# A two-layer hybrid decoder step on one core: token groups of 512, 512 and 64 in both MLPs instead of 384, 384 and 320

## What is computed

```python
x = x + m                                  # m: the token mixer's output
h = rmsnorm(x, norm_mlp[layer])
x = x + jnp.square(jax.nn.relu(h @ w_up[layer])) @ w_down[layer]
```

## Time and profile before

| | before |
|---|---|
| median of 3 runs | 2856.1 us |
| span of the profiled execution | 2853.2 us |
| TensorE matmul busy | 2650.3 us, 93% |
| TensorE weight load busy | 2527.7 us, 89% |
| VectorE busy | 1397.6 us, 49% |
| GpSimd busy | 852.2 us, 30% |
| ScalarE busy | 629.0 us, 22% |
| mean granted TensorE clock | 0.951 of full |

### The profile page before, as it was taken

The page is one execution under the profiler, slowest core; times in us unless marked ns, Lnnn a source line. Parts: engine busy times, 40 slices in busy tenths (PEclk is TensorE's granted clock), DMA queues, the critical chain, the costliest instruction groups (busy, mean ns, idle before and its releaser), DMA issues.

```text
span 2853.2 us, 38633 instructions
## 1 busy us (share of the span) xinstructions
PE 2650.3 (93%) x15232; PEld 2527.7 (89%) x15232; DVE 1397.6 (49%) x2168; ACT 629.0 (22%) x1086; POOL 852.2 (30%) x383
## 2 busy tenths in 40 slices
PE   5988987999999999998989999897999999999996
PEld 5978756999999999998978888787999999999996
DVE  3656444643443344346566767653643443344344
ACT  3050124130110011003232525342220110011002
POOL 2332101433333333333211111112433333333331
PEclk9999978999999999999979999887999999999998
DMA  3111002111111111112101111102111111111111
GB/s 119 40 31 53 23 24 100 45 38 45 45 45 45 45 45 45 45 45 77 60 24 45 40 37 40 39 30 100 45 38 45 45 45 45 45 45 45 45 45 70
DMA packets 36849, 137.63 MB, mean 48 GB/s; under 512 B 5697, under 2 KB 6337, under 8 KB 35409
## 3 DMA queue, kind: packets, MB, share of 16 engines
q1 hardware_dynamic: 28368, 103.56, 10.9%
q10 hardware_dynamic: 8320, 31.70, 2.9%
HBM read 120.36 MB, written 14.88 MB: 47 GB/s over the span
## 4 chain that ended last, share of the span: by engine, by line
issue 55%; PE 29%; POOL 14%; DVE 1%; POOLq 1%; DMA 0%; ACT 0%; DVEq 0%; ACTq 0%; SPq 0%
PE PS L457 29%; POOL WH L437 8%; POOL WL L440 6%; DVE X L1533 0%; DMA WR<-ws 0%; DVE RA L1119 0%; POOLq L436 0%; POOLq L448 0%; DVE X L1129 0%; POOLq L439 0%; ACT RS L784 0%; DVE RS L1082 0%; ACT L787 0%; ACT L784 0%; PE PS L507 0%
## 5 line engine op out<-in xcount | busy, mean ns | idle before, releaser
L457 PE MATMUL PS<-RA,WH 128*128 128x384 f32 (+1 forms) x4800 | 1182.5, 330 | 71.4 <-DVE RA L1073 23.9
L457 PE MATMUL PS<-RB,WH 128*128 128x384 f32 (+1 forms) x4272 | 1063.4, 332 | 12.4 <-DVE TR L1115 8.6
L437 POOL TENSOR_TENSOR WH<-WR,ZERO 128x1024 fp32r<-128x1024 f32 x189 | 362.3, 1917 | 1941.6 <-PE PS L457 1938.1
L457 PEld LDWEIGHTS PS<-RA,WH 128*128 128x128 f32 x4800 | 853.1, 189 | 84.1 <-issue 69.2
L457 PEld LDWEIGHTS PS<-RB,WH 128*128 128x128 f32 x4272 | 765.8, 191 | 27.7 <-issue 21.0
L457 PE MATMUL PS<-RA,WL 128*128 128x384 f32 (+1 forms) x2400 | 787.4, 328 | 0.0
L457 PE MATMUL PS<-RB,WL 128*128 128x384 f32 (+1 forms) x2136 | 704.1, 330 | 0.0
L440 POOL TENSOR_TENSOR WL<-WR,WH 128x1024 fp32r<-128x1024 f32 x189 | 489.6, 2591 | 14.8
L457 PEld LDWEIGHTS PS<-RA,WL 128*128 128x128 f32 x2400 | 454.0, 189 | 0.0
L1129 DVE TENSOR_TENSOR X<-PS,X 128x384 f32<-128x384 f32 (+1 forms) x384 | 202.4, 534 | 468.0 <-PE PS L457 468.0
L457 PEld LDWEIGHTS PS<-RB,WL 128*128 128x128 f32 x2136 | 407.0, 191 | 0.0
(11 more groups left out here) (178 smaller groups left out, 1621.2 us busy)
## 6 DMA issues: line engine op xcount, KB each, us to landing
WR<-ws SPq DMA_DIRECT2D x189, 512.0 KB, 3.3
X<-xT ACTq DMA_DIRECT2D x8, 544.0 KB, 8.8
EB<-xT ACTq DMA_DIRECT2D x8, 544.0 KB, 7.9
x_spill<-X ACTq DMA_DIRECT2D x1, 4352.0 KB, 13.1
EB<-x_spill ACTq DMA_DIRECT2D x8, 544.0 KB, 7.1
yT<-X SPq DMA_DIRECT2D x8, 544.0 KB, 2.7
GA<-st_gla ACTq DMA_DIRECT2D x4, 1024.0 KB, 5.6
glas_o<-GA ACTq DMA_DIRECT2D x4, 1024.0 KB, 3.9
```

The lines of the kernel that those rows point to most:

```text
L437: nc.gpsimd.tensor_tensor(WH[:, slot, :], WR[:, slot, :], ZERO[:, 0:1].to_broadcast([P, 1024]), ALU.add).then_inc(w_high, 1)
L457: return nc.tensor.matmul(out, lhsT, rhs, start=start, stop=stop, skip_group_check=True)
```

## The change

A second table is added and used in the MLPs alone: by TensorE in up and down steps (a new parameter `cut` of `group`, `step` and `first_step`), by ScalarE in its square and its copy, and by VectorE in `up` and `down`. The mixers, the 1/rms factor and the final norm stay with `GROUPS`. Three groups, three banks and all semaphore counts stay. In the first up step of an MLP VectorE waits for all three parts of 1/rms before its first group, since the first 512 columns span two parts.

```diff
 GROUPS = [(0, 384), (384, 384), (768, T - 768)]
+MLP_GROUPS = [(0, 512), (512, 512), (1024, T - 1024)]
...
-            def group(n, slot, g, src, tiles, w0, o=0, two=False, after_two=False, signal=2):
+            def group(n, slot, g, src, tiles, w0, o=0, two=False, after_two=False, signal=2, cut=GROUPS):
...
-                s, size = GROUPS[g]
+                s, size = cut[g]
...
-                            first_step(n, RB, parts_of, norm)
+                            first_step(n, RB, parts_of, norm, cut=MLP_GROUPS)
                         else:
-                            step(n, slot, RB, after_two=after_two)
+                            step(n, slot, RB, after_two=after_two, cut=MLP_GROUPS)
...
-                                  o=o, two=True, after_two=after_two or j > 0, signal=1)
+                                  o=o, two=True, after_two=after_two or j > 0, signal=1, cut=MLP_GROUPS)
...
-                        A(TR[:, grp(g)], TR[:, grp(g)], ACT.Square).then_inc(sq_done, 1)
+                        A(TR[:, s:s + size], TR[:, s:s + size], ACT.Square).then_inc(sq_done, 1)
...
-                    for g, (s, size) in enumerate(GROUPS):
+                    for g, (s, size) in enumerate(MLP_GROUPS):
                         if first:
-                            dve.wait_ge(rs_ready, 3 * (norm - 1) + g + 1)
+                            dve.wait_ge(rs_ready, 3 * norm)
...
-                        for g, (s, size) in enumerate(GROUPS):
+                        for g, (s, size) in enumerate(MLP_GROUPS):
                             dve.wait_ge(gemm_done, 6 * n + 3 * o + g + 1)
```

More of the change, by code:

```diff
@@ L474, in group, with step, first_step @@
                 last.then_inc(gemm_done, signal)
-            def step(n, slot, src, after_two=False):
+            def step(n, slot, src, after_two=False, cut=GROUPS):
                 for g in range(3):
-                    group(n, slot, g, src, range(KT), 0, after_two=after_two)
-            def first_step(n, src, f, norm=None, after_two=False, order=range(KT)):
+                    group(n, slot, g, src, range(KT), 0, after_two=after_two, cut=cut)
+            def first_step(n, src, f, norm=None, after_two=False, order=range(KT), cut=GROUPS):
                 slot = n % 2
@@ L486, in first_step @@
                     pe.wait_ge(h_low, 8 * f + at + 1)
-                    for g, (s, size) in enumerate(GROUPS):
+                    for g, (s, size) in enumerate(cut):
                         if at == 0 and n:
@@ L798, in one @@
                 def one(n, v, tile):
-                    for g, (s, size) in enumerate(GROUPS):
+                    for g, (s, size) in enumerate(MLP_GROUPS):
                         act.wait_ge(psum_free, 6 * n + 2 * (g + 1))
-                        A(TR[:, grp(g)], TR[:, grp(g)], ACT.Square).then_inc(sq_done, 1)
+                        A(TR[:, s:s + size], TR[:, s:s + size], ACT.Square).then_inc(sq_done, 1)
                         act.wait_ge(sq_done, v + (g + 1))
-                        A(RA1[:, 0, tile, s:s + size], TR[:, grp(g)], ACT.Copy).then_inc(a_high, 1)
+                        A(RA1[:, 0, tile, s:s + size], TR[:, s:s + size], ACT.Copy).then_inc(a_high, 1)
                 v0 = 96 * layer
@@ L1114, in up @@
                             dve.wait_ge(a_low, v - 2 + g)
-                        V.scalar_tensor_tensor(TR[:, grp(g)], PS[:, g, 0:size], 0.0, RS[:, s:s + size],
+                        V.scalar_tensor_tensor(TR[:, s:s + size], PS[:, g, 0:size], 0.0, RS[:, s:s + size],
                                                ALU.max, ALU.mult).then_inc(psum_free, 2)
-                    for g, (s, size) in enumerate(GROUPS):
+                    for g, (s, size) in enumerate(MLP_GROUPS):
                         dve.wait_ge(a_high, v + g + 1)
-                        V.tensor_tensor(RA1[:, 1, tile, s:s + size], TR[:, grp(g)],
+                        V.tensor_tensor(RA1[:, 1, tile, s:s + size], TR[:, s:s + size],
                                         RA1[:, 0, tile, s:s + size].bitcast(F32), ALU.subtract).then_inc(a_low, 1)
```

## The result

| | before | after |
|---|---|---|
| median | 2856.4 us (4 runs, 2855.9 to 2857.5) | 3074.4 us (4 runs, 3073.8 to 3075.7) |
| ratio, 95% interval | | 1.0765 [1.075, 1.0779] |
| span of the profiled execution | 2853.2 us | 3072.0 us |
| granted TensorE clock, mean | 0.951 | 0.954 |

The change makes the kernel 218 us slower. The forecast was 3076.0 us, 1.6 us above the median.

The account below looks back on a forecast made before the run. TensorE was taken to bound the MLPs, 1514 of 2853 us. Span 2853.2 + 221.2 (short matmuls) + 1.8 (wait) - 2.6 (tail) - 0.5 (last evictions) = 3073.1 us; median 2.9 above, 3076.0; range 3050 to 3125.

Parts of the forecast that it names:

- Columns plus 13.3 ns: TensorE in the MLPs: a matmul costs its columns at 2.4 GHz plus 13.3 ns, unless something slower stands behind it.
- The short matmul: 64-column group in the MLPs: an exposed weight load makes each matmul 112 ns, not 40; 3072 of them, +221.2 us.
- The wait: First up step of each MLP: group 0's eviction waits for all three Exp, TensorE resumes 0.9 us later; +1.8 us.
- The tail's waits: First MLP's tail: two TensorE waits of 1.13 us on VectorE would be gone, up to 1.3 us each, -2.6 us.
- that margin: Down steps: TensorE needs bank 0 again after 6.78 us, 5.94 before; margin grows by 0.8 us, counted as no gain.
- The clock: Rival, short groups of up steps: the clock falls to half, 206 ns per matmul, +144 us more, 3220 us; 6%.
- Loads hidden or cheaper in float32r: Rival, 64-column group: 40 ns per short matmul, 2855 us, 4%; half way, some 67 ns, 2938 us, another 4%.
- faster long matmuls: Rival, 512-column matmuls: the 13.3 ns vanish or shrink; 2773 us with loads hidden, 2994 us with them exposed; 2%.
- the upper bound of 120 ns: 64-column matmul in the MLPs: at most the load and then 13.3 ns on top, +246.7 us.
- Float32r in four passes: Rival, short matmuls: done as float32 with two loads, 224 ns, 3419 us; without a second load 120 ns; 4%.

Follow-up runs that it names:

- the half-load run: The changed kernel, but matmuls of the 64-column group use 64 of their 128 weight columns, except in `first_step`: 2930.2 us, 1.0259 of before.
- the low parts' run: The kernel before, with each low part of an up step written behind the next group's eviction, the last at the end: 2850.8 us, 0.9984 of before.
- the 128- and 192-column cuts: The changed kernel with groups of 512, 448 and 128 columns: 2998.3 us, 1.0499 of before; with 448, 448 and 192: 2924.0 us, 1.0242.

## Why the prediction was right

*The bound and the formula.* TensorE's spacing set the time before and after. Columns plus 13.3 ns held from 256 to 512 columns (120, 147, 173, 187 and 227 ns at 256, 320, 384, 416 and 512), but for the 203 ns at 448.

*The short matmul.* The one term that carried the sum was the 112 ns of a load, taken from float32 loads behind 64 and 8 columns and one pair of float32r loads behind an idle array. Measured: 111 to 112 ns. Half-width loads in rows 6 had said that it was the load; the half-load run showed it for float32r. 3072 x 72 = 221 us stands against 218.8 us of span in all.

*The small terms.* The wait was right, 0.77 + 0.13 us twice. The tail's waits, which the prediction wanted gone, are not; they shrank from 1.13 us to 0.38:

```profile
1421.81 0.74 PE L458 MATMUL PS<-RA,WH 128*128 128x512 f32 x2 [0.38 <-DVE X L1130]
1436.01 0.73 PE L458 MATMUL PS<-RA,WH 128*128 128x512 f32 x2 [0.38 <-DVE X L1130]
```

Two times 0.75 in place of 2.6 us: the allowance of up to 1.3 each was too large, more than the wait of rows 10 and more than the 0.84 us of slack that were to take it away. What I left out works the other way: the fourteen short waits for bank 0 in down steps, which the kernel before has and the changed one, needing the bank 0.8 us later, does not. The prediction named that margin, and took it as worth nothing; the low parts' run put it at up to 4.6 us. Against it stand the turns of the loops, where TensorE's idle time grew from 3.8 us in four turns to 5.1 and the clock fell at two of these turns (below). These errors of 1 to 5 us partly cancel, and that the forecast came as near as 1.6 us to the median is luck to that extent.

*VectorE.* Its busy time grew by 1.7% (1397.6 to 1421.5 us), where under 1% was forecast. Evictions were right (692 ns for 512 columns, 224 for 64; 675 and 250 were forecast). The 512-column low parts lasted 2521 ns on average beside GpSimd's splits. Nothing followed from it.

*The clock.* In the main this rival is refuted: the stretches were granted 0.99 and 1.00 with 64-column groups in every step. A trace of it is there. The first row is TensorE's resumption after a turn of the loop in the first MLP; the stretch around it was granted 0.83, the next 14 us full clock again:

```profile
1059.19 0.73 PE L458 MATMUL PS<-RB,WH 128*128 128x512 f32 x2 [1.43 <-issue]
...
1056.00:1066.00 10.00, 8.57 (x38) 7.01 (x37) 0.92 (x2) 0.00 (x0) 4.26 (x2) 0.83 0.18 56
1066.00:1080.00 14.00, 14.00 (x76) 12.03 (x75) 6.60 (x6) 3.04 (x6) 4.62 (x2) 1.00 0.01 1
```

A short group and then 1.43 us of idle time stood before this drop. They do not bring it every time: at the turn before, at 839.97 us, 1.42 us of idle time stood behind a short group too, and the stretch of 838 to 852 us was granted full clock. The second drop is in the second MLP (0.76 from 2443 to 2449 us). By an estimate from the 0.83 over 10 us, such a drop costs 1.7 us.

*The other rivals.* Loads hidden or cheaper in float32r, and faster long matmuls, would have shown spacings of 40 or 67 ns, or long ones under 227; neither was there. A load and then the 13.3 ns on top, the upper bound of 120 ns, was not there either. Float32r in four passes is out by the half-load run and by the 128- and 192-column cuts.

*The skill's rule.* By the Trainium skill's page "TensorE: Matmul & The Clock Gate", section "Back-to-back issue gap", 64 columns would have followed each other in about 25 ns, which by its own words leaves the loads out. The trace has 112. The same page's section "LDWEIGHTS (loading the stationary operand)" gives a load's time as its columns divided by 1.2 GHz; an estimate from it is 107 ns for 128 columns and 53 for 64. The trace comes near to that with 112 and 58. Where every matmul brought its own weights, as here, the second rule decided.

## What to carry to other kernels

Where each matmul has its own 128-wide float32r weights and TensorE sets the time at full clock, a matmul of fewer than about 236 columns costs as much as one of 236 (112 ns less 13.3, times 2.4 columns per ns; an estimate, since 192 and 256 columns are the sizes measured on either side). Cut the token columns so that the shortest group stays above that. Beyond it, how they are cut made little difference (2864.1 us with groups of 512, 320 and 256, against 2856.1), so filling banks to 512 gains nothing when the number of groups stays. Ask of every uneven cut what its remainder costs, not what its large pieces save. And read the spacing of starts: the busy share of TensorE was 93% with and without the loss.

## What the runs showed of the hardware

- A load is hidden only under the matmul right before its own: alternating 512- and 64-column matmuls took 343 ns a pair, and 3084.0 us in all against 3074.4 in blocks.
- Float32r loads go with the weights' width: 58 ns for 64 columns, 112 for 128, at full clock.
- 448-column matmuls had a mean spacing of 203 ns, where 416 (187) and 512 (227) lie on the line of columns plus 13.3 ns. Why is open.
- VectorE's float32r low part of 384 columns took 0.55 us when it was written before the up step's end (1098.74 us in the run with early low parts) and 2264 ns on average in the kernel before, where all stand behind it, beside GpSimd's split. Moving one of three ahead left the sum of their times as it was (315.7 and 320.7 us) and still gained 4.6 us: the time at which VectorE was through counted.
